# Expert gather with the down and up tables side by side: one 8 KB row per step

## The reference, cut to what matters

```python
a = jnp.einsum("tkd,td->tk", peer_down[ee], hh)   # dot product with each chosen down row
act = gg * jax.nn.gelu(a)                          # gate times activation
out = jnp.einsum("tk,tkd->td", act, peer_up[ee])   # weighted sum of the chosen up rows
```

## Time and profile before

| | |
|---|---|
| time, median of 3 runs (lowest to highest) | 4179.11 us (4178.96 to 4184.13) |
| span of the profiled execution, first to last instruction | 4362.9 us |
| busy share of the span: PE, DVE, POOL, ACT | 77%, 59%, 47%, 19% |
| moved | 1330.31 MB, mean 305 GB/s |
| mean granted TensorE clock | 0.867 of 2.4 GHz |

### The profile page before, as it was taken

One profiled execution on the slowest core, in us unless ns is written; L12 is line 12 of the kernel. 1 busy time (PEld: TensorE's weight loads), 2 busy tenths in 40 slices (PEclk: granted clock), 3 DMA queues, 4 the chain that ended last, 5 costly groups with the idle time before them and its releaser, 6 DMA issues.

```text
span 4362.9 us, 35889 instructions
## 1 busy us (share of the span) xinstructions
PE 3358.4 (77%) x11238; PEld 1715.0 (39%) x11238; DVE 2577.2 (59%) x5454; ACT 816.5 (19%) x1926; POOL 2040.9 (47%) x2148
## 2 busy tenths in 40 slices
PE   6889686888767787887687766766878887866766
PEld 2357442356434243551354422221366654422111
DVE  1412768566686846676357674666563347684776
ACT  1311111321211122121211111111231211111111
POOL 0210566655555666666116665566000005676665
PEclk9999899999979899996899988866988998999556
DMA  6663998999999999999849999999400039999999
GB/s 228 227 237 130 338 363 320 375 356 409 401 362 355 343 378 352 392 410 375 298 159 369 333 365 392 372 405 374 157 1 1 1 113 338 352 350 372 379 369 346
DMA packets 380787, 1330.31 MB, mean 305 GB/s; under 512 B 39500, under 2 KB 44876, under 8 KB 377016
## 3 DMA queue, kind: packets, MB, share of 16 engines
q0 software_dynamic: 313344, 1141.10, 69.3%
q1 hardware_dynamic: 61104, 164.18, 10.1%
q10 hardware_dynamic: 6152, 22.74, 1.4%
HBM read 1326.69 MB, written 1.17 MB: 304 GB/s over the span
## 4 chain that ended last, share of the span: by engine, by line
PE 15%; DVE 10%; DMA 9%; issue 7%; POOL 5%; another core or an unknown queue 3%; ACT 2%; ACTq 0%; DVEq 0%; POOLq 0%
PE ps L1701 15%; POOL arena L3075 5%; DMA arena<-in_peer_up,arena 5%; DVE arena L893 3%; DVE arena L906 3%; DMA arena<-in_peer_v,arena 2%; ACT arena L2462 1%; DMA arena<-in_ada_w 1%; DMA arena<-in_peer_u,arena 1%; DMA arena<-in_peer_down,arena 1%; PE ps L1707 1%; DVE arena L914 1%; DVE arena L1287 1%; DVE arena L1282 0%
## 5 line engine op out<-in xcount | busy, mean ns | idle before, releaser
L1701 PE MATMUL ps<-arena 128*128 128x512 f32 (+9 forms) x10500 | 3254.6, 490 | 873.9 <-ACT arena L2462 231.9
L1701 PEld LDWEIGHTS ps<-arena 128*128 128x128 f32 (+4 forms) x10500 | 1621.6, 196 | 2435.2 <-issue 1844.2
L906 DVE SCALAR_TENSOR_TENSOR arena<-arena,ps 128x1024 f32<-128x1024 f32 x1024 | 1240.6, 1217 | 542.1 <-DMA arena<-in_peer_down,arena 289.1
L3075 POOL DMA_INDIRECT arena<-in_peer_down,arena x768 | 747.1, 973 | 654.8 <-DVE arena L910 269.5
L3075 POOL DMA_INDIRECT arena<-in_peer_up,arena x768 | 736.5, 959 | 541.2 <-PE ps L1701 294.3
L2462 ACT ACTIVATE arena<-arena 128x128 f32<-128x128 f32 (+5 forms) x1242 | 444.4, 387 | 1890.8 <-PE ps L1701 636.3
L3075 POOL DMA_INDIRECT arena<-in_peer_u,arena x256 | 248.4, 970 | 647.9 <-DVE arena L910 543.6
L906 DVE SCALAR_TENSOR_TENSOR ps<-arena,ps 128x512 f32<-128x512 f32 x508 | 383.4, 755 | 143.0 <-DMA arena<-in_peer_up,arena 88.8
L2462 ACT ACTIVATE arena<-ps 128x512 f32<-128x512 f32 (+4 forms) x349 | 191.5, 549 | 1165.6 <-PE ps L1701 547.9
L3075 POOL DMA_INDIRECT arena<-in_peer_v,arena x256 | 242.4, 947 | 149.2 <-issue 59.9
L893 DVE TENSOR_TENSOR arena<-arena 128x512 f32<-128x512 f32 (+8 forms) x398 | 246.9, 620 | 72.1 <-ACT arena L2462 42.1
(11 more groups left out here) (34 smaller groups left out, 565.1 us busy)
## 6 DMA issues: line engine op xcount, KB each, us to landing
arena<-in_w_mod POOLq DMA_DIRECT2D x40, 1024.0 KB, 6.6
arena<-in_gate_blocks SPq DMA_DIRECT2D x16, 2048.0 KB, 7.8
arena<-in_w_in SPq DMA_DIRECT2D x14, 2048.0 KB, 7.9
arena<-in_w_pq SPq DMA_DIRECT2D x13, 2048.0 KB, 16.0
arena<-in_ada_w POOLq DMA_DIRECT2D x24, 1024.0 KB, 8.3
arena<-in_w_out SPq DMA_DIRECT2D x8, 2048.0 KB, 8.0
arena<-in_gate_blocks SPq DMA_DIRECT2D x8, 1792.0 KB
arena<-mod_scratch ACTq DMA_DIRECT2D x26, 512.0 KB
```

Of the source, the lines that this page charges most:

```text
L906: self.e.scalar_tensor_tensor(o, a, s, b, op0, op1, accum_out=accum).then_inc(*(inc or self.inc(self.S.vec)))
L1701: return self.e.matmul(o, l, r, start=start, stop=stop)
L3075: self.e.indirect_dma_start(out=o, out_offset=None, in_=table, in_offset=bass.IndirectOffsetOnAxis(ap=idx.bitcast(U32), axis=0)).then_inc( ...
```

## The change

The two tables are stored side by side on the host, so that a row of the new table holds the down row and then the up row of one expert (2048 floats, 8 KB). POOL issues one indirect transfer per step, into one of `NR` = 6 buffers of 8 KB per partition, `K.pairs`, and waits only for TensorE's last product on the buffer that it reuses. `LAG` is 1. ScalarE takes each step's column by itself: GELU, times the gate (a Copy with the gate as scale), then the diagonal; for that it waits for VectorE's dot product of the step. A new semaphore, `gated`, tells it that the gates are there. TensorE multiplies both halves of the up row in every tile; VectorE keeps only the dot product. `fold` uses the modulation row as its temporary. The buffers move in SBUF, the arena grows by 1536 floats per partition, and the scratch for the descriptors of POOL's transfers goes from 8192 to 2048 bytes. Three holds of the work behind (`("after", ...)`) get other step numbers.

```diff
-ND = NU = 5
+NR = 6
 GK = 16
-LAG = GK + 2
+LAG = 1
...
+    def pair(self, s):
+
+        x = self.base + s
+        return self.K.pairs[x % NR], (self.S.pair_in[x % NR], 16 * (x // NR + 1))
...
-            yield ("after", 2 * NEXT + LAG + 2)
+            yield ("after", 2 * NEXT + 14)
...
-            yield ("after", NEXT + LAG + 2)
+            yield ("after", NEXT + 16)
...
# Vector.gather
-                d, there = self.down_place(s)
+                buf, there = self.pair(s)
                 self.wait_ge(*there)
+                d = buf[:, 0:1024]
                 self.stt(d, d, 1.0, K.HP, M, M, inc=self.inc(S.down), free=True, accum=K.AA[n % 2][:, k:k + 1])
-            if s >= GK + 1 and (s - 1) % GK == 0 and s - 1 <= total:
...
-                self.tt(w[:, ks], w[:, ks], K.GT[:, tiles[n_], ks], M, inc=self.inc(S.weighted), free=True)
...
-                    self.stt(K.av, src, w, K.av, M, AD, inc=self.inc(S.up_vector), free=True)
...
# Vector.fold
-        self.tt(K.tpb, K.ap, gr[:, 0:512], M)
-        self.tt(self.X(t)[:, 0:512], self.X(t)[:, 0:512], K.tpb, AD)
-        self.tt(K.tpb, K.av, gr[:, 512:1024], M, inc=self.inc(S.sum_read))
-        self.tt(self.X(t)[:, 512:1024], self.X(t)[:, 512:1024], K.tpb, AD, inc=self.inc(S.tile_done))
+        self.tt(gr[:, 0:512], K.ap, gr[:, 0:512], M)
+        self.tt(gr[:, 512:1024], K.av, gr[:, 512:1024], M, inc=self.inc(S.sum_read))
+        self.tt(self.X(t), self.X(t), gr, AD, inc=self.inc(S.tile_done))
...
# Tensor.gather
-                ins = self.mm(K.ap, K.dg[c % 4], buf[:, 0:512], k == 0, k == NEXT - 1)
-                if n % 2 == 0:
-                    ins = self.mm(K.av, K.dg[c % 4], buf[:, 512:1024], k == 0, k == NEXT - 1)
+                ins = self.mm(K.ap, K.dg[c % 4], buf[:, 1024:1536], k == 0, k == NEXT - 1)
+                ins = self.mm(K.av, K.dg[c % 4], buf[:, 1536:2048], k == 0, k == NEXT - 1)
...
# Scalar.gather
-                self.wait_ge(S.down, base + s)
-                self.act(K.AW[n_ % 2][:, ks], K.AA[n_ % 2][:, ks], gelu, inc=self.inc(S.activated))
...
+                if k in K.routed_at[tiles[n]]:
+                    self.wait_ge(*self.next(S.gated))
+                self.wait_ge(S.down, c + 1)
+                self.act(w, K.AA[n % 2][:, k:k + 1], gelu, inc=self.inc(S.activated), free=True)
+                self.act(w, w, ACT.Copy, scale=K.GT[:, tiles[n], k:k + 1], inc=self.inc(S.weighted))
                 if c >= 4:
                     self.wait_ge(S.up_tensor, c - 3)
-                self.act(K.dg[c % 4], K.ident, ACT.Copy, scale=K.AW[n % 2][:, k:k + 1], inc=self.inc(S.diagonal), free=True)
+                self.act(K.dg[c % 4], K.ident, ACT.Copy, scale=w, inc=self.inc(S.diagonal))
...
# Pool.gather
-                if s >= ND:
-                    self.wait_ge(S.down, c - ND + 1)
...
-                self.fetch(o, down, K.EI[:, tiles[n], k:k + 1], there[0])
...
-                self.fetch(o, up, K.EI[:, tiles[n], k:k + 1], there[0])
+                self.freed(max(0, s - NR + 1))
+                o, there = self.pair(s)
+                self.fetch(o, table, K.EI[:, tiles[n], k:k + 1], there[0])
...
# layout, kernel
+    f["peer_rows"] = np.concatenate([np.asarray(inputs["peer_down"]), np.asarray(inputs["peer_up"])], 2).reshape(2 * 16384, 2 * D)
...
-    nc = bacc.Bacc("TRN2", target_bir_lowering=False, num_devices=1, dynamic_dma_scratch_size=8192)
+    nc = bacc.Bacc("TRN2", target_bir_lowering=False, num_devices=1, dynamic_dma_scratch_size=2048)
```

More of the change, by code:

```diff
@@ L147, in __init__ @@
         self.rows, self.units = 0, 0
-        self.base, self.shared, self.gathers = 0, 0, 0
+        self.base = 0
         self.halves_in = 0
@@ L284, in until @@
         return done
-    def halves(self, u):
-        return self.shared + sum(min(max(0, u - n * NEXT), NEXT) for n in (1, 3))
     def units_of(self, n):
@@ L485, in peer_topk, with gather @@
         yield from self.peer_pick(l, t, m, 0, 8)
-    def gather(self, tiles, tables, gelu, rows):
+    def gather(self, tiles, table, gelu, rows):
         total = NEXT * len(tiles)
@@ L588, in main @@
         zpair = lambda who: K.H2[:, 2 * who:2 * who + 2, 0:928]
-        tables, gelu, gelu2 = (A["peer_down"], A["peer_up"]), ACT.Gelu_apprx_tanh, ACT.Gelu
+        table, gelu, gelu2 = A["peer_rows"], ACT.Gelu_apprx_tanh, ACT.Gelu
         def temps(mem):
@@ L717, in main @@
         done = self.until(queries, (0, 0))
-        self.weave(self.gather([0, 1, 2, 3], tables, gelu, [(0, 0, 5), (0, 0, 5), (0, 1, 5), (0, 1, 5)]),
+        self.weave(self.gather([0, 1, 2, 3], table, gelu, [(0, 0, 5), (0, 0, 5), (0, 1, 5), (0, 1, 5)]),
                    ctx_then_x(queries), RATE0, done=done)
@@ L762, in queries_then_second @@
             self.second_asked()
[L763 removed]
+            yield ("after", NEXT + 14)
             self.second_vectors()
[L765 removed]
+            yield ("after", NEXT + 16)
             self.folded(5)
@@ L769, in queries_then_second @@
                 yield from self.z_block(0, j)
-        self.weave(self.gather([0, 1], tables, gelu, [(1, 0, 5), (1, 0, 5)]), queries_then_second(queries), RATE1, done=done)
+        self.weave(self.gather([0, 1], table, gelu, [(1, 0, 5), (1, 0, 5)]), queries_then_second(queries), RATE1, done=done)
         self.folded(6)
@@ L1393, in gather @@
         self.base += total
-        self.shared += total // 2
-        self.gathers += 1
     def fold(self, t, c, n0, gr, g_in):
@@ L3028, in modhalf, with gather @@
         yield from self.units_of(2)
-    def gather(self, tiles, tables, gelu, rows):
+    def gather(self, tiles, table, gelu, rows):
         K, S = self.K, self.S
         base, total = self.base, NEXT * len(tiles)
-        down, up = tables
         for s in range(total + LAG):
@@ L3261, in memory @@
     K.sums = [K.wbuf[2][:, 0:2048], K.wbuf[2][:, 2048:4096], arena[:, NB:NB + 2048]]
-    gm = Mem(arena, (GR, K.BG))
-    more = Mem(arena, (NB, NB + 2 * D))
-    K.ds, K.us = [gm(D) for _ in range(ND - 1)] + [more(D)], [gm(D) for _ in range(NU - 1)] + [more(D)]
-    K.dg, K.AA, K.AW = [gm(128) for _ in range(4)], [gm(128) for _ in range(2)], [gm(128) for _ in range(2)]
-    K.tpb = gm(512)
+    gm = Mem(arena, (G0, K.BG))
+    K.pairs = [gm(2 * D) for _ in range(NR - 1)] + [arena[:, NB:NB + 2 * D]]
+    K.dg = [gm(128) for _ in range(4)]
+    more = Mem(arena, (NB + 2 * D, NB + 2 * D + 1536))
+    K.EI, K.GT = more(4, 128, dt=I32), more(4, 128)
+    K.AA, K.AW = [more(128) for _ in range(2)], [more(128) for _ in range(2)]
     K.HP, K.ap, K.av = K.psum[:, 0:1024], K.psum[:, 1024:1536], K.psum[:, 1536:2048]
```

103 lines of the change are left out of this document (19 added, 84 removed).

## The result

The changed kernel takes 4313.9 us (median of four runs, 4313.43 to 4316.68) against 4179.03 for the kernel before (4172.66 to 4184.13): 1.032 times as long, interval 1.0304 to 1.0335. The forecast was 4160 us in a range of 4060 to 4265. It is slower by 3.2%, and outside the range.

A forecast was written before the change was run, and what follows sets the result against it. Transfers were taken as the bound, 2.80 us per bare step. On the profiled 4362.9 us, -19 -10 -38 +30 +5 +13 = -19 gave 4344, times 0.958 about 4160 us; range 4110 to 4200 for its own case, 4060 to 4265 overall.

The forecast's parts named there:

- ScalarE, and the chain of a step: ScalarE's activations per step: no cost by volume, but more table loads around single GELUs, +13 us (0 to 59).
- Rings and waits: Six-buffer ring: 15.4 us less 5.8 to the dot and 4.3 of chain leaves 5.3 us slack; no cost charged.
- Rival C: Chain on the ring: query products and their evictions delay steps, no gain in even tiles; +82, 4258 us; chance 0.24.
- TensorE in odd tiles: TensorE takes the up row's second half: second tile +30 us, fourth +5, sixth fits, eighth nothing.
- The transfers: One 8 KB row for two of 4 KB: bare step 2.80 to 2.65 us; eighth tile -19, sixth -10, even -38.
- rival B: Larger rows run at the densest rate, 418 GB/s, bare step 2.5 us; -146, 4040 us; chance 0.20.
- Rival D: 8 KB rows go at the pace of 4 KB, 2.80 us per bare step; +71, 4247 us; chance 0.10.
- the scratch at nothing: The smaller scratch for POOL's transfer descriptors costs nothing; if it held fewer fetches than the ring, 2.9 us per step.
- 1.28 us a load: ScalarE's function table loads cost 1.28 us each, without the drain that would make it 2.66.
- the clock in the last tile: TensorE's granted clock near 0.96 in the last tile with both halves, so its second product costs nothing there.
- TensorE as the bound of the second tile: With 122 us more, TensorE needs 462 of 420 us in the second tile and becomes its bound.
- The fold at nothing: The fold waits for the tile's last product, 2 to 3 us eight times, covered by the 5.3 us slack.

The follow-up runs named there:

- both edits: The changed kernel with a plain copy for each step's GELU and the up row's second half in odd tiles back on VectorE: 4179.29 us.
- the chain out: The changed kernel with copy for GELU, odd tiles' second half on VectorE, and the diagonal made from the gate alone, TensorE waiting for the row itself: 4125.97 us.
- the second trace: The kernel before, unchanged, profiled once more: it spans 4172.1 us.
- the two-transfer run: The changed kernel with two transfers of 4 KB rows per step, from separate tables into the same buffer, for one of 8 KB: 4366.74 us.

## Why the prediction was wrong

The parts, each undone or done alone: the longer row -53; whole rows on TensorE +53 to +62; the loads +87; the chain without loads +53. The sum is +140 to +149 us; 135 were measured. By estimate some 12 us of the 87 belong to the 53 loads that the kernel before has as well, at the 0.22 us that a load costs there; without them the sum is +128 to +137. By stretch, products and loads alone come within 5 us of what was measured: 20 us at the gather's start and 27 of loads in the first tile (+48.8), 25 of products and 25 of loads in the second (+50.5), 28 and 26 less the 20 at the gather's end in the fourth's stretch (+29.2). The longer row's -53 and the chain's +53 about cancel.

**The step that failed is "ScalarE, and the chain of a step", at +13 us (0 to 59), for which the runs show 87, by estimate 75 more than in the kernel before.** The count was good for the tile that it looked at (60 loads estimated in the second tile, 58 there), but "the other tiles have fewer" was not looked up: the first has 37 and the fourth 48, as the views below and the 163 loads above show. And the price was taken as ScalarE's busy time, which has room, where it is a delay in a chain that each of six buffers waits for. The trace has the mechanism at 952 us in the second tile:

```profile
951.68 2.53 PE L1662 MATMUL ps<-arena 128*128 128x256 f32 x7
...
952.52 0.47 ACT L2420 ACTIVATE arena<-ps,arena 128x256 f32<-128x256 f32 x1 [3.27 <-PE ps L1662]
...
953.01 1.28 ACT L2420 ACT_TABLE_LOAD   x1
...
954.31 1.94 ACT L2420 ACTIVATE arena<-arena 128x1 f32<-128x1 f32 x6
954.48 0.94 POOL L3005 DMA_INDIRECT arena<-in_peer_rows,arena  x1 [4.25 <-PE ps L1662]
...
955.39 1.13 PE L1662 MATMUL ps<-arena 128*128 128x512 f32 x2 [1.18 <-ACT arena L2420]
```

A row joins instructions that follow each other without a break: of TensorE's seven from 951.68, three belong to the work behind, and from 952.33 on the four of the gather's step before, which end at 954.21. ScalarE's sigmoid at 952.52 stands ahead of the gather's next steps in its order, and ScalarE had been idle for 3.27 us until the products that it reads were there; then come the load, 1.28 us, and six activations, the three of each of two steps. TensorE waits 1.18 us for the first of their diagonals; begun at 953.01, three activations of 0.32 us would have had it ready at 953.98, before TensorE was free. POOL's 4.25 us of idle time before the fetch at 954.48 are another delay on the same ring: TensorE had been at the products of the work behind, and the buffer came free when its gather products ended at 954.21. In the first gather TensorE's idle time divides as follows, in the kernel before and in the changed one:

```profile
L1701 PE MATMUL ps<-arena 128*128 128x512 f32 (+6 forms) x4248 | 1385.3, 497 | 285.3 <-DMA arena<-in_peer_up,arena 164.5 <-ACT arena L2462 81.5 <-DMA arena<-in_ada_w 23.9
```

```profile
L1662 PE MATMUL ps<-arena 128*128 128x512 f32 (+8 forms) x4760 | 1549.0, 497 | 261.2 <-ACT arena L2420 224.8 <-DMA arena<-in_ada_w 19.9 <-DVE arena L880 7.0
```

What ended with ScalarE rose from 81.5 to 224.8 us. It is 169.6 without GELU; it is 233.3 with both edits, where TensorE has less to do, and 57.8 there with the chain out. Among the longest waits of the changed kernel in the first gather are these:

```profile
POOL arena L3005 <- PE ps L1662: 1166.2, 503, 9.5
...
PEld ps L1662 <- ACT arena L2420: 426.2, 279, 18.3
...
DVE arena L893 <- DMA arena<-in_peer_rows,arena: 303.9, 183, 7.9
```

where the columns are us in total, times and longest. POOL waits for TensorE 503 times in 512 steps, and the dot 304 us for transfers. These totals are not the loads' alone: without GELU they are 1084.9, 360.8 and 350.7 us. Loads by tile, in the first, the second and the fourth:

```profile
L2420 ACT ACT_TABLE_LOAD x37 | 47.5, 1283 | 7.6 <-DVE arena L893 5.9
```

```profile
L2420 ACT ACT_TABLE_LOAD x58 | 74.4, 1283 | 8.5 <-PE ps L1662 5.4
```

```profile
L2420 ACT ACT_TABLE_LOAD x48 | 61.6, 1283 | 2.6
```

**"Rings and waits" named the slack and then charged nothing for it.** The 5.3 us were right as a length (the chain measures 4.33 us, the shortest time from issue to landing 5.2), and wrong as cover: one buffer less costs 65 us, the chain taken out returns 53. Slack was taken as used by one delay at a time; but delays come one after the other: loads at 944.66, 947.97, 953.01 and 957.26 us, and between them TensorE's products of the work behind, from 948.85 to 952.33. That the ring has no time to refill in between is argued from this, and no run shows it by itself. Rival C had this mechanism and a sum of 4258, with 4313.9 measured; it put the cost into the bursts of query products alone, and gave it 0.24. Its sign, POOL waiting for TensorE while TensorE waits for ScalarE, is what the traces show.

**TensorE in odd tiles: mis-sized in the fourth.** +30 for the second tile (25 measured on the kernel before), +5 for the fourth (28 from its first dot to the next gather's). The clock did rise as expected, in the second tile from 0.93 to 0.99 and in the fourth's stretch from 0.87 to 0.95; even so the product cost 28 us there, nearer to the upper end (36) than to the 5.

**The transfers: right in kind and near in size.** -67 us were forecast in three terms (19 + 10 + 38), -53 measured as a whole, at 0.08 us per bare step instead of 0.15: in the second trace the bare step had been 2.59 us and not 2.80, so there was less to win. The bound of 2.51 us was reached (2.51, at 419 GB/s), which had been rival B's sign. The estimate of 1.2% from the Trainium skill ("DMA: Bandwidth & Descriptors", Why small descriptors are slow) is less than the 2.3% from 2.57 to 2.51. Rival D and the sum of rival B are excluded by the two-transfer run: the row's gain is real, and it isn't 146 us.

**Right:** the scratch at nothing, as far as it was tried, the clock in the last tile, TensorE as the bound of the second tile, and 1.28 us a load: the activation at 954.31 begins 0.02 us after the load's end, and the load 0.02 us after the sigmoid's. The 2.66 us that the Trainium skill ("ScalarE: Activation LUTs", What ACT_TABLE_LOAD costs) has for a load with its drain are not seen here: behind 125 of the 196 loads the next activation begins within 0.1 us. The fold at nothing was not tried by itself.

What stays open: single runs give each part to some 10 us, so the sum of the parts tells nothing finer. What a chain costs in the kernel before, with its 18 steps of lag, was not measured, and how the 25 us of the loads at that lag divide between ScalarE's time and the evictions wasn't tried. No version beat the kernel before. The run with the chain out, which leaves the dot product out of the result, is 53 us below it; as two activations per step are gone there as well, it doesn't give by itself what a larger distance between fetch and use would be worth. More than six buffers of 8 KB were not tried.

## What to carry to other kernels

Before a lag between two engines is given up for a smaller buffer or a longer transfer, price the chain that then turns a buffer over, with everything that stands ahead of its steps in each engine's order; an engine that is idle two thirds of the time can still be the one for which all wait. A function that alternates with others on ScalarE is worth its batch of 16: count the switches that single steps would cause in every stage, not in the one that looks worst.

## What the hardware showed

Rows of 8 KB instead of two of 4 KB gave 419 GB/s for 409 in the bare steps (409 in the two-transfer run too), at a DMA share of 1.01 and 1.03, so the share alone hides such a gain. A load of a function table took 1.28 us, and ScalarE's next activation began 0.02 us behind it. TensorE's granted clock was 0.56 in bare steps with one product per 2.59 us and 1.00 with two: the second product cost almost no time there (193.8 us busy for 183.4).
